# A two-block transformer kernel with a stream of experts: TensorE's pieces of projections and mixers ahead of each step's value products

## The chip, the cores and the metric

The kernel runs on one core of one Trainium2 chip. The metric is the device time of one execution in microseconds; three runs of the kernel before gave 2456.52 to 2461.20 us, with a median of 2458.12.

A core has five engines with instruction queues of their own: TensorE (PE), VectorE (DVE), ScalarE (ACT), GpSimd (POOL) and SyncE (SP). They meet through semaphores. Each executes its own program in order, so an instruction that waits holds up everything behind it on its engine.

## What is computed

Two blocks follow each other on 256 tokens of width 1024. The first mixes a convolution and a recurrent layer, the second has two layers, one with gated linear attention (GLA) and one with stick-breaking attention (SB), both with an attention over a memory of 256 rows. Each of the three layers ends in a PEER layer: 8 heads choose 16 of 16384 experts for each token, and each expert is a pair of rows u and v.

```python
q = (xb @ w_q).reshape(TOK_BLOCK, PEER_HEADS, 2, PEER_DHALF)
s = jnp.einsum('thcd,hcnd->thcn', q, sub_keys).astype(jnp.float32)
top_s, top_i = lax.top_k(s, K)
...
u = expert_u[e]
act = jax.nn.gelu(jnp.einsum('td,ted->te', xb, u), approximate=False)
coef = (gate * act.astype(jnp.float32)).astype(xb.dtype)
return jnp.einsum('te,ted->td', coef, expert_v[e])
```

Everything is float32. The chosen rows of u and v are different for every token, so they are gathered: 128 tokens x 128 experts x 8 KB for each half of the tokens and each layer, 805 MB over the three layers.

## The kernel before

After a first phase (`one_tensor` and its like, up to about 300 us) the kernel runs the *stream*: 768 experts, one after the other, in 384 *steps* of two (`GROUP`). 64 steps make a *window* (`WINDOW`): one layer for one half of the tokens. There are six, counted here from 0: windows 0 and 1 are the first block's layer, 2 and 3 the GLA layer's, 4 and 5 the SB layer's. "Step 23 of window 3" is step 3 x 64 + 23 of the stream.

An expert goes through these stations:

- GpSimd gathers u and v of its 128 tokens (1 MB) into one of eight ring slots (`RING`), once the slot's last user is done: `pool.wait_ge(sem("v_used"), e - RING + 1)`, L2086.
- VectorE multiplies u with the tokens and adds up (the dot product, L2007).
- ScalarE takes GELU (L2053), multiplies with the gate (L2059) and writes the coefficient on the diagonal of a 128x128 matrix (L2065, semaphore `diag`), one of four buffers (`DIAGS`), which it may fill once the products of two steps before are done.
- TensorE multiplies the diagonal with the two halves of v and adds to two accumulators (L1977), then counts up `v_used`, which frees the slot. One step is four instructions, of which the trace shows each as two.

*Beside* the stream runs everything that makes the next layer ready: in window w the mixer of the half whose experts were just added, the projection of the queries, and the scores. `beside_tensor`, `beside_vector` and `beside_scalar` are generators that give a slot number ahead of each piece, and `Beside.run(s)` issues all pieces whose number is at most s. Each engine calls it in its own step s: VectorE behind the dot products of the step, ScalarE behind the diagonals, TensorE behind the products. So the slot numbers set the order, and pieces of one number on two engines can wait for each other. `late` is a second such generator, for the first window alone.

In a mixer's window with first slot `base`, what matters here is:

- SB mixer (windows 3 and 4): `memory_tensor` writes the memory's scores into two banks at slot 20, ScalarE's `memory_exp_scalar` (L2254, four exponentials) reads them at slot 23, and TensorE's `values_part(0)` (L1611, weights `in_sb_v`), also at slot 23, takes the same two banks for its output. `sb_scores_tensor` and `sb_above_tensor` (L2714, L2725, L2728) stand at slot 21 for the third group of heads, and ScalarE copies the scores out at slot 22.
- Queries (`queries_tensor`, all of windows 1 to 4): projection j (L1599) at slot 46 + j, ScalarE's copy of it (L1586) one slot later; the scores of a group of keys (L1743) stand in the slot of the copy of the group's last query.
- Row broadcasts (`row_tensor`, L1472), which the layer norms read: at slot 0 of windows, and at step 380 for the last norm.
- At the start of a window VectorE adds the accumulators to the residual (L1525, `peer_added`), and the first products of the window wait for it.
- Softmax of the best scores (L2023 on ScalarE, behind its pieces in every eighth step), which VectorE needs for the gate (L2214).

TensorE works through six further banks (0 to 5) in turn. `banks.take` waits until the bank's last content has been read. Weights come through three slots that SyncE reloads once TensorE has used them.

Of the kernel before, what the change touches and what calls it, by code (L numbers as in the profile page):

```python
# [203 lines left out]
def build(nc, io):  # L204
    with ExitStack() as ctx:  # L205
# [5 lines left out]
        def sem(name):  # L211
            if name not in sems:
                sems[name] = ctx.enter_context(nc.semaphore(name))
            return sems[name]
# [109 lines left out]
        for n in range(len(plan)):  # L324
            s = n % SLOTS if n < stream_from else (n - stream_from) % STREAM_SLOTS
# [1449 lines left out]
        def late_tensor(pe):  # L1775

            for group in range(EARLY_GROUPS):
                lo, hi = FIRST_GROUPS[group]
                for j in range(lo, hi):
                    for part in range(2):  # L1780
                        yield late_slot(group, 2 * (j - lo) + part)
                        if part == 0:
                            pe.wait_ge(*banks.take(("q", 0, j, 1)))
                        out = banks.bank(("q", 0, j, 1))
                        for kc in range(4 * part, 4 * part + 4):
                            ins = nc.tensor.matmul(out[:, 0:P], early_q[:, j, kc * P:(kc + 1) * P], xT[:, kc, cols_of(1)],
                                                   start=kc == 0, stop=kc == KC - 1)
                    ins.then_inc(banks.full_sem(("q", 0, j, 1)), 1)
                yield late_slot(group, 4)
                for j in range(lo, hi):  # L1790
                    pe.wait_ge(*banks.emptied(("q", 0, j, 1)))
                early_scores(pe, group, 1, late_q)
# [171 lines left out]
        def stream_tensor(pe):  # L1964
            beside = Beside(beside_tensor(pe))
            late = Beside(late_tensor(pe))
            beside.run(-1)
            pe.wait_ge(sem("w_o_last_added"), 2)
            for s in range(UNITS // PH * WINDOW):
                if s and s % WINDOW == 0:  # L1970
                    pe.wait_ge(sem("peer_added"), 2 * (s // WINDOW))
                for e in range(s * GROUP, (s + 1) * GROUP):
                    first, last = e % TILE_EXPERTS == 0, e % TILE_EXPERTS == TILE_EXPERTS - 1
                    pe.wait_ge(sem("diag"), e + 1)
                    for half, acc in enumerate((acc_lo, acc_hi)):
                        at = D + 512 * half
                        ins = nc.tensor.matmul(acc[:, :], diag[:, e % DIAGS, :], ring[:, e % RING, at:at + 512],  # L1977
                                               start=first, stop=last)
                        if e == UNITS * PK - 1 and half == 0:
                            ins.then_inc(sem("last_half"), 1)  # L1980
                    ins.then_inc(sem("v_used"), 1)
                beside.run(s)
                late.run(s)
            beside.run(UNITS * PK)

        def stream_vector(v):
# [104 lines left out]
        def beside_tensor(pe):  # L2091
            yield from first_tensor(pe)
            for w in range(4):
                n, i = w // NT + 1, w % NT
                yield from (gla_tensor, sb_tensor)[n - 1](pe, i, WINDOW * (w + 1))
                yield from queries_tensor(pe, n, i, WINDOW * (w + 1))
            for i in range(NT):
                yield WINDOW * (5 + i) - 4 * i
                for which in range(2):
                    row_tensor(pe, 5, i, which)  # L2100
# [813 lines left out]
        @blk.tensor  # L2914
        def _(pe):
            one_tensor(pe)
            stream_tensor(pe)
# [142 lines left out]
```

## Time and profile before

| | us |
|---|---|
| median of three runs | 2458.12 |
| the profiled execution, its time | 2457.63 |
| its span, first to last instruction | 2455.8 |
| TensorE busy (matmul) | 2215.1 |
| VectorE busy | 1663.9 |
| ScalarE busy | 904.5 |
| GpSimd busy | 879.6 |

Busy times are shares of a span in which the engines work beside each other; they can't be added. The gathers take 78.5% of what sixteen DMA engines could do in the span, the loads of weights 13.4%. "PE" is the matrix product and "PEld" the loading of its stationary operand, which lies beside it. In a timeline each row is a run of equal instructions: start, length, engine, line, operation, and in brackets the idle time of the engine ahead of it with what ended it. A granted clock of 1.00 is TensorE at 2.4 GHz, and 0.5 would be 1.2 GHz throughout.

### The profile page before, as it was taken

The page shows a single profiled execution, that of the slowest core. Times are in us where ns is not written, and L with a number is a line of the kernel's source. Part 1 is how long each engine was busy: PE and PEld are TensorE (multiplying, and loading weights), DVE is VectorE, ACT ScalarE, POOL GpSimd, SP SyncE. Part 2 cuts the span into 40 slices and gives each one's busy share as a digit, 9 for nine tenths or more (in the row PEclk, how much of TensorE's full clock was granted, in tenths as well). Part 3 has the DMA queues.
Part 4 walks back from the last instruction along what each step waited for, and adds up shares of the span by engine and source line. Part 5 has one row for each costly group of instructions (what it writes and reads, how often), then busy time and mean ns, then how long its engine had stood idle before and what let it go on. Part 6 is the DMA issues. An engine that isn't in the chain of part 4 may idle for free. (4 is left out here: it accounts for less than half of the span.)

```text
span 2455.8 us, 29961 instructions
## 1 busy us (share of the span) xinstructions
PE 2215.1 (90%) x9826; PEld 1270.1 (52%) x9826; DVE 1663.9 (68%) x3980; ACT 904.5 (37%) x2654; POOL 879.6 (36%) x796
## 2 busy tenths in 40 slices
PE   9989999989998889998989987899999999977777
PEld 7877755544554435654545644445655445622223
DVE  3864576666675677666777656767678767676765
ACT  2232133332343434343443424424344534433332
POOL 0012044444433334433344432344443344444442
PEclk9999999999999999999999999999999999999999
DMA  5321699999999999999999999999999999999997
GB/s 198 129 70 33 247 379 426 426 426 427 426 424 424 415 418 412 412 425 424 419 402 426 425 425 422 396 423 426 418 425 422 389 422 426 400 420 427 427 427 323
DMA packets 149784, 934.90 MB, mean 381 GB/s; under 512 B 16656, under 2 KB 18800, under 8 KB 51200
## 3 DMA queue, kind: packets, MB, share of 16 engines
q0 software_dynamic: 110592, 805.36, 78.5%
q1 hardware_dynamic: 39040, 127.65, 13.4%
q8 instruction: 79, 1.29, 0.2%
q14 instruction: 73, 0.60, 0.1%
HBM read 931.89 MB, written 1.05 MB: 380 GB/s over the span
## 5 line engine op out<-in xcount | busy, mean ns | idle before, releaser
L1977 PE MATMUL bank<-arena 128*128 128x512 f32 x3072 | 1425.2, 608 | 196.6 <-ACT arena L2065 193.3
L2086 POOL DMA_INDIRECT arena<-in_uv,idx x768 | 851.9, 1109 | 1359.3 <-PE bank L1977 1218.3
L1977 PEld LDWEIGHTS bank<-arena 128*128 128x128 f32 x3072 | 566.5, 193 | 889.2 <-issue 582.3
L2007 DVE CUSTOM_DVE_ANT_0 arena<-arena,h 128x1024 f32<-128x1024 f32 x512 | 627.4, 1226 | 351.0 <-DMA arena<-in_uv,idx 346.9
L2053 ACT ACTIVATE arena<-arena 128x2 f32<-128x2 f32 x383 | 77.8, 203 | 1046.8 <-DVE arena L2007 1046.3
L2007 DVE CUSTOM_DVE_ANT_0 arena<-arena 128x1024 f32<-128x1024 f32 x256 | 313.8, 1226 | 192.5 <-DMA arena<-in_uv,idx 190.9
L2065 ACT ACTIVATE arena<-const,arena 128x128 f32<-128x128 f32 x766 | 260.0, 386 | 2.2 <-PE bank L1977 2.2
L378 PEld LDWEIGHTS bank<-xT,weights 128*128 128x128 f32 x1360 | 196.5, 191 | 40.6 <-issue 23.5
L378 PE MATMUL bank<-xT,weights 128*128 128x128 f32 (+2 forms) x1360 | 214.8, 314 | 0.0
L2059 ACT ACTIVATE arena<-arena 128x1 f32<-128x1 f32 x766 | 184.3, 288 | 12.5
L1586 ACT ACTIVATE arena<-bank 128x128 f32<-128x128 f32 (+4 forms) x158 | 46.9, 306 | 172.6 <-PE bank L1599 115.3
L2053 ACT ACT_TABLE_LOAD x73 | 93.7, 1283 | 1.3
L1388 POOL TENSOR_TENSOR arena<-arena 128x512 f32<-128x512 f32 (+1 forms) x16 | 17.9, 1125 | 190.5 <-DVE arena L1206 162.9
L2007 DVE DVE_READ_ACCUMULATOR2_ANT arena<- 128x1 f32 x768 | 63.2, 82 | 0.0
L2023 ACT ACT_TABLE_LOAD x48 | 61.6, 1283 | 0.8
L1611 PE MATMUL bank<-weights,xT 128*128 128x256 f32 (+1 forms) x128 | 47.8, 503 | 15.2 <-DMA weights<-in_sb_v 9.4
L1611 PE MATMUL bank<-weights,arena 128*128 128x512 f32 x128 | 60.0, 594 | 0.0
L1108 DVE SCALAR_TENSOR_TENSOR arena<-arena,rows 128x256 f32<-128x256 f32 x120 | 47.6, 478 | 0.0
L1611 PEld LDWEIGHTS bank<-weights,xT 128*128 128x128 f32 x128 | 23.6, 192 | 43.4 <-issue 22.5
L2214 DVE RECIPROCAL arena<-arena 128x1 f32<-128x1 f32 x48 | 7.8, 163 | 54.9 <-ACT arena L2023 54.7
L617 PE MATMUL bank<-arena 64*64 64x64 f32 (+1 forms) x1104 | 37.2, 218 | 6.0 <-DVE arena L1234 4.9
L1599 PEld LDWEIGHTS bank<-xT,held 128*128 128x128 f32 x320 | 38.6, 192 | 7.7 <-issue 7.7
(349 smaller groups left out, 1994.5 us busy)
## 6 DMA issues: line engine op xcount, KB each, us to landing
weights<-in_w_in SPq DMA_DIRECT2D x38, 512.0 KB, 3.5
weights<-in_a_fm SPq DMA_DIRECT2D x28, 512.0 KB, 8.8
arena<-in_uv,idx POOLq DMA_INDIRECT x768, 13.1
arena<-in_w_q SPq DMA_DIRECT2D x16, 512.0 KB, 14.7
weights<-in_w_q SPq DMA_DIRECT2D x16, 512.0 KB, 8.7
weights<-in_a_out SPq DMA_DIRECT2D x16, 512.0 KB, 8.6
weights<-in_b_fm SPq DMA_DIRECT2D x16, 512.0 KB, 8.9
weights<-in_b_out SPq DMA_DIRECT2D x16, 512.0 KB, 8.1
```

The costliest lines, as they stand in the source:

```text
L378: ins = nc.tensor.matmul(out[:, 0:n], w[:, kc * P:(kc + 1) * P], x[:, kc, :], start=kc == 0, stop=kc == KC - 1)
L1108: V.scalar_tensor_tensor(ycv[:, c, :], glu[:, c, bass.ds(tap + META, TOK)], cols[:, bass.ds(tap * CT + (w0 + c), 1)], ycv[:, c, :], ALU.mu ...
L1586: nc.scalar.activation(to, out[0:to.shape[0], 0:n], ACT.Copy, scale=scale).then_inc(banks.emptied_sem(job), 1)
L1599: ins = nc.tensor.matmul(out[:, 0:P], w[:, kc * P:(kc + 1) * P], xw[:, kc, :], start=kc == 0, stop=kc == KC - 1)
L1611: ins = nc.tensor.matmul(banks.bank((name, i, half))[:, 0:hw], x, slot((name, i, kc))[:, 512 * half:512 * half + hw], start=first, stop=last)
L1977: ins = nc.tensor.matmul(acc[:, :], diag[:, e % DIAGS, :], ring[:, e % RING, at:at + 512], start=first, stop=last)
L2007: V.tensor_tensor_reduce(out=u, in0=u, in1=x, scale=1.0, scalar=0.0, op0=ALU.mult, op1=ALU.add, accum_out=dots[:, unit % 2, kx:kx + 1]).th ...
L2023: ins = nc.scalar.activation(expo, best, ACT.Exp, bias=tiny[:, 0:1], accum_out=tiny[:, 1:2])
L2053: nc.scalar.activation(actv[:, par, kx:kx + GROUP], dots[:, par, kx:kx + GROUP], ACT.Gelu).then_inc(sem("gelu"), 1)
L2059: nc.scalar.activation(coef[:, par, j:j + 1], actv[:, par, j:j + 1], ACT.Copy, scale=gate[:, par, j:j + 1]).then_inc(sem("coef"), 1)
L2065: nc.scalar.activation(diag[:, (e + j) % DIAGS, :], ident, ACT.Copy, scale=coef[:, par, kx + j:kx + j + 1]).then_inc(sem("diag"), 1)
L2086: nc.gpsimd.indirect_dma_start(out=ring[:, s, :], out_offset=None, in_=io[f"uv{unit // PH // NT}"], in_offset=bass.IndirectOffsetOnAxis(ap ...
```

## The change

In each step of `stream_tensor` the two calls that issue the pieces move from behind the products to the head of the step, ahead of the wait for `peer_added` too. The other engines' programs stay as they are.

```diff
@@ -1967,6 +1967,8 @@
             beside.run(-1)
             pe.wait_ge(sem("w_o_last_added"), 2)
             for s in range(UNITS // PH * WINDOW):
+                beside.run(s)
+                late.run(s)
                 if s and s % WINDOW == 0:
                     pe.wait_ge(sem("peer_added"), 2 * (s // WINDOW))
                 for e in range(s * GROUP, (s + 1) * GROUP):
...
                     ins.then_inc(sem("v_used"), 1)
-                beside.run(s)
-                late.run(s)
             beside.run(UNITS * PK)
```

The products' line is L1977 before and L1979 after. On TensorE around step 23 of window 3, before: the last two instructions of the products of step 22, those of step 23, the first values piece, and the first half of the products of step 24.

```order
L1977 MATMUL bank<-arena 128x512 [waits diag]
L1977 MATMUL bank<-arena 128x512
L1977 MATMUL bank<-arena 128x512 [waits diag]
L1977 MATMUL bank<-arena 128x512
L1977 MATMUL bank<-arena 128x512 [waits diag]
L1977 MATMUL bank<-arena 128x512
L1611 MATMUL bank<-weights,xT 128x512 [waits emptied_4,landed_2]
L1611 MATMUL bank<-weights,xT 128x256 [waits emptied_5]
L1611 MATMUL bank<-weights,xT 128x512 [waits landed_0]
L1611 MATMUL bank<-weights,xT 128x256
L1977 MATMUL bank<-arena 128x512 [waits diag]
L1977 MATMUL bank<-arena 128x512
```

The same place after: the end of the products of step 22, the first values piece, the products of step 23, and the start of the second values piece.

```order
L1979 MATMUL bank<-arena 128x512 [waits diag]
L1979 MATMUL bank<-arena 128x512
L1611 MATMUL bank<-weights,xT 128x512 [waits emptied_4,landed_2]
L1611 MATMUL bank<-weights,xT 128x256 [waits emptied_5]
L1611 MATMUL bank<-weights,xT 128x512 [waits landed_0]
L1611 MATMUL bank<-weights,xT 128x256
L1979 MATMUL bank<-arena 128x512 [waits diag]
L1979 MATMUL bank<-arena 128x512
L1979 MATMUL bank<-arena 128x512 [waits diag]
L1979 MATMUL bank<-arena 128x512
L1611 MATMUL bank<-weights,xT 128x512 [waits landed_1]
```

The piece with its waits for `emptied_4` and `emptied_5`, which ScalarE's exponentials (L2254) count up, has moved ahead of the products of its step.

On TensorE from the end of window 4 into window 5, before: the scores piece behind the last products of window 4, the first products of window 5, and the row broadcasts for the norm.

```order
L1743 MATMUL bank<-weights,arena 128x128 [waits emptied_3,emptied_4,emptied_2,emptied_5,emptied_1,landed_0]
L1743 MATMUL bank<-weights,arena 128x128 x3
L1977 MATMUL bank<-arena 128x512 [waits diag,peer_added]
L1977 MATMUL bank<-arena 128x512
L1977 MATMUL bank<-arena 128x512 [waits diag]
L1977 MATMUL bank<-arena 128x512
L1472 MATMUL bank<-row_parts,const 128x128 [waits emptied_0,rows_in]
L1472 MATMUL bank<-row_parts,const 128x128 x3
L1472 MATMUL bank<-row_parts,const 128x128 [waits emptied_1]
L1472 MATMUL bank<-row_parts,const 128x128 x3
```

The same place after.

```order
L1743 MATMUL bank<-weights,arena 128x128 [waits emptied_3,emptied_4,emptied_2,emptied_5,emptied_1,landed_0]
L1743 MATMUL bank<-weights,arena 128x128 x3
L1979 MATMUL bank<-arena 128x512 [waits diag]
L1979 MATMUL bank<-arena 128x512
L1979 MATMUL bank<-arena 128x512 [waits diag]
L1979 MATMUL bank<-arena 128x512
L1472 MATMUL bank<-row_parts,const 128x128 [waits emptied_0,rows_in]
L1472 MATMUL bank<-row_parts,const 128x128 x3
L1472 MATMUL bank<-row_parts,const 128x128 [waits emptied_1]
L1472 MATMUL bank<-row_parts,const 128x128 x3
```

The scores now stand ahead of the last products of window 4, and the row broadcasts ahead of the first of window 5, which still wait for `peer_added`.

## Rows read from the trace of the kernel before

**Rows 1.** Page, 40 slices: busy tenths of PE and DMA, and GB/s.

```profile
PE   9989999989998889998989987899999999977777
...
DMA  5321699999999999999999999999999999999997
GB/s 198 129 70 33 247 379 426 426 426 427 426 424 424 415 418 412 412 425 424 419 402 426 425 425 422 396 423 426 418 425 422 389 422 426 400 420 427 427 427 323
```

**Rows 2.** Table of waits, whole run: total us, times, longest us.

```profile
POOL arena L2086 <- PE bank L1977: 1218.3, 698, 7.2
...
PE bank L1977 <- ACT arena L2065: 193.3, 163, 4.6
...
ACT arena L1586 <- PE bank L1599: 115.3, 62, 3.8
```

**Rows 3.** Gathers (L2086) of 2160:2400, then 1550:1595, 1925:1965, 2090:2150.

```profile
DMA to landing us min/median/max: 11.4/12.6/14.8
...
DMA to landing us min/median/max: 6.8/10.8/14.2
...
DMA to landing us min/median/max: 6.3/8.1/10.4
...
DMA to landing us min/median/max: 5.9/8.4/11.7
```

**Rows 4.** Windows: length, busy PE PEld DVE ACT POOL, clock, DMA share, GB/s.

```profile
1570.00:1600.00 30.00, 28.48 (x101) 14.36 (x102) 17.55 (x45) 11.33 (x32) 8.87 (x9) 1.00 0.97 368
1900.00:1960.00 60.00, 57.20 (x196) 29.67 (x194) 47.79 (x105) 32.43 (x79) 20.36 (x17) 0.97 0.97 387
2110.00:2160.00 50.00, 46.88 (x191) 27.02 (x190) 39.49 (x97) 20.24 (x64) 20.84 (x20) 1.00 0.99 385
2049.28:2135.23 85.95, 85.47 (x402) 54.67 (x400) 56.46 (x141) 32.43 (x109) 35.65 (x33) 1.00 1.00 412
```

**Rows 5.** Timeline of PE, steps 22 to 26 of window 3.

```profile
1539.82 3.70 PE L1977 MATMUL bank<-arena 128*128 128x512 f32 x8 [0.28 <-ACT arena L2065]
1545.67 5.40 PE L1977 MATMUL bank<-arena 128*128 128x512 f32 x8 [2.16 <-ACT arena L2065]
1550.91 2.74 PE L1611 MATMUL bank<-weights,xT 128*128 128x512 f32 x8
1553.49 3.60 PE L1977 MATMUL bank<-arena 128*128 128x512 f32 x8
...
1559.62 1.56 PE L1611 MATMUL bank<-weights,xT 128*128 128x512 f32 x4 [1.24 <-DMA weights<-in_sb_v]
1561.01 3.60 PE L1977 MATMUL bank<-arena 128*128 128x512 f32 x8
1566.59 1.56 PE L1611 MATMUL bank<-weights,xT 128*128 128x512 f32 x4 [1.99 <-DMA weights<-in_sb_v]
...
1571.38 3.60 PE L1977 MATMUL bank<-arena 128*128 128x512 f32 x8
```

**Rows 6.** Timeline of ACT, window 3: last of four exponentials at step 23.

```profile
1548.59 0.48 ACT L2254 ACTIVATE arena<-bank,small 128x256 f32<-128x256 f32 x1
```

**Rows 7.** Windows, L1977 alone: length, busy PE PEld, clock, DMA share, GB/s.

```profile
1545.60:1551.10 5.50, 5.40 (x8) 2.03 (x8) 0.69 1.01 426
```

**Rows 8.** Timeline of PE, window 2, behind a longer wait.

```profile
1237.53 9.45 PE L1977 MATMUL bank<-arena 128*128 128x512 f32 x16 [4.59 <-ACT arena L2065]
```

**Rows 9.** Timeline of ACT, window 4, step 22: copies of the scores.

```profile
1904.24 1.09 ACT L1586 ACTIVATE arena<-bank 128x512 f32<-128x512 f32 x2 [4.61 <-PE bank L2714]
```

**Rows 10.** Timelines of DVE and PE, end of window 4 and start of 5.

```profile
2105.49 0.16 DVE L2214 RECIPROCAL arena<-arena 128x1 f32<-128x1 f32 x1 [5.44 <-ACT arena L2023]
...
2138.77 3.73 PE L1472 MATMUL bank<-row_parts,const 80*128 80x128 f32 x32
```

**Rows 11.** Timeline of PE, the last three steps.

```profile
2437.41 10.46 PE L1977 MATMUL bank<-arena 128*128 128x512 f32 x24
```

**Rows 12.** Timeline of PE, window 0, piece of step 2.

```profile
340.66 1.10 PE L394 MATMUL bank<-xT,weights 128*128 128x256 f32 x4 [0.72 <-DVE xT L1578]
```

## The prediction

> **What bounds the kernel now.** I read the page first, by its slices. Over almost the whole stream of experts the DMA engines are busy in every slice and move about 426 GB/s; TensorE shows nine tenths or more in most slices beside them [rows 1]. The table of waits says how they hang together: a gather waits for TensorE's product (L1977) 698 times, and the product waits for ScalarE's diagonal (L2065) for 193.3 us in all [rows 2]; between the two lies VectorE's dot product. It is a ring of eight slots, so two things can set the end: the bytes, or the ring, when TensorE releases a slot so late that the DMA queue runs empty.
>
> Which one it is can be read from a gather's time from issue to landing. In the last window, where TensorE has no other work, it is 11.4 to 14.8 us and the slices move 427 GB/s: the queue is full, bytes are the bound. Where the rate falls, the time does too: 6.8 to 14.2 us from 1550 to 1595, 6.3 to 10.4 from 1925 to 1965, and 5.9 to 11.7 from 2090 to 2150 [rows 1, 3]. I take 8 us, near the low ends and the median of 8.1 in the leanest stretch, as the time of a gather that finds no queue ahead of it; what a stretch shows above that is its cover, the time by which a release may come late at no cost. The three stretches in which the rate falls most move 368 GB/s over 30 us, 387 over 60 and 385 over 50 [rows 4]. Against 427 that is 30 x 59/427 = 4.1 us, 60 x 40/427 = 5.6 us and 50 x 42/427 = 4.9 us: some 15 us are lost to the ring, and no more can be won there. A later release costs time only where cover is gone, and there it costs nearly its own length.
>
> **What the change does to TensorE.** Nothing is added or removed, and the other four engines keep their rows. In the program, each step's pieces now stand behind the products of the step before and ahead of its own. Since products and pieces alternate either way, most steps look alike: TensorE did pieces s-1 and then waited for diagonal s; now it does pieces s in the same gap. Two things differ. First, ahead of products s there now lies piece s instead of piece s-1, so where TensorE has no idle time, products s start later by (piece s minus the piece that last fell into idle time), and earlier where the next piece is short. Second, ScalarE does its own part of step s behind diagonal s. A piece that needs that part used to have 3.6 us of products as cover; now TensorE stands still for it with the products queued behind, and the release of two slots behind them. By the semaphores I find such pieces at steps 22 of windows 1 and 2, at 20, 23 and 27 of windows 3 and 4, at the five groups of scores in each of windows 1 to 4, and at five places of window 0. The other way round, ScalarE's copy of step s+1 no longer waits for products s.
>
> **The sum, place by place.** Times are of the profiled execution (span 2455.8, its time 2457.63; the median of the three runs is 2458.12, so I add 0.5).
>
> *Window 3, step 23.* The value projection's first piece takes the two banks that ScalarE's four exponentials of the memory read. These run behind the diagonal of step 23 and end at 1548.59 + 0.48 = 1549.1. The products before end at 1539.82 + 3.70 = 1543.5, and the diagonal is ready when the next start, at 1545.67 [rows 5, 6]. Now TensorE stands until 1549.1, does the piece (2.74 us), and the products start near 1551.8, 6.1 us later, and end at 1555.4 instead of 1551.1. The pieces behind it are long: from the end of one step's products to the start of the next 3.9 us (1557.1 to 1561.0) and 6.8 us (1564.6 to 1571.4), with waits of 1.24 and 1.99 us for weights in them [rows 5]. They now lie ahead of products 24 and 25 instead of 25 and 26. Carrying the times forward so gives releases later by 4.3, 5.7, 8.6, 7.1, 4.5 and 2.7 us for steps 23 to 28. The weights' own chain (use, reload, use) moves with the pieces, which I have counted as half of its waits saved. Cover at these steps, each gather's time to landing less 8 us, is about 5, 5, 6, 3, 1 and 0 us; its two ends are those of the stretch [rows 3]. So the queue runs dry by 0, 1, 3, 4, 3.5 and 3: **3.5 us**, not given back, since from there the bytes bind again.
>
> The clock adds to it. The eight product records took 5.40 us there, behind 2.16 us of idle, and 3.6 a step later; the granted clock of that stretch is 0.69, so a part of it went at 1.2 GHz, for 1.8 us more. Behind 4.59 us of idle in window 2 sixteen records took 9.45 us instead of 7.2, 2.25 more [rows 5, 7, 8]. The new idle time is 5.6 us, and the piece behind it goes at the low clock too, so I take up to 2 us more and half of it as reaching the end: **1 us**. The Trainium skill (TensorE: Matmul & The Clock Gate, "Why this matters for your kernels") wants no long idle gaps of TensorE between bursts, since its clock goes back to half rate behind one. If only the new, longer gap counted as one, the whole 1.8 us would be new and the term 1.8; the row shows the fall at 2.16 us of idle time already, and I go by the row.
>
> *Window 4, the same step.* Here ScalarE itself waited 4.61 us for TensorE's scores of the step before, and its copies came at 1904.24 [rows 9]. That piece now goes ahead of its products, so ScalarE is about 3 us earlier, its exponentials end near 1908.5, and TensorE arrives at that time: no stall. What is left is the order: releases later by 3, 6, 2.4, 4.4, 4, 1.4 and 3.2 us, cover 3, 4, 0.5, 2, 0.5, 0 and 0. Carried through, **1.7 us**.
>
> *End of window 4.* From 2049.28 to 2135.23 TensorE is busy for 85.47 of 85.95 us: in this stretch it sets the pace, in either order [rows 4]. The last idle time before it lies at a step with a short piece, so the 1.6 us piece of each step now comes ahead of its products and releases move back by 1.0 us. Behind the window's end the four broadcasts of the norm's rows (3.4 us) precede the first products instead of following them: that release is 2.4 us later, the next 1.1 us earlier [rows 10]. Cover is nil there: **1 us**. VectorE's 5.44 us wait for the softmax (it came because ScalarE's copy stood behind a piece that stood behind products) goes away, but TensorE is late there by more [rows 10]; nothing is gained.
>
> *The start.* Piece 2 of window 0 waits for VectorE's transposes, in place at 340.66 [rows 12]; its products now start near 341.5 instead of 336.3. The ring has just been filled there, and a release 5 us late uses its cover up to within 1 us; I take **0.3** (0 to 1.5). The five score groups of window 0, and those of windows 1 and 2 with step 22, stall TensorE by 1 to 5 us, over cover of 4 us or more and with idle time behind them: nought, at most 1 us in all.
>
> *The tail.* The norm rows (3.4 us) stood behind the products of step 380 and left the last three steps back to back, 2437.41 to 2447.87 [rows 11]. Now they use 1.2 us of idle time ahead of them; only the last expert's diagonal, ready by 2445.0, binds: **-0.6 us**.
>
> Sum: 3.5 + 1 + 1.7 + 1 + 0.3 - 0.6 = 6.9, so 2457.63 + 6.9 + 0.5 = **2465.0 us**. The uncertain terms reach from nothing to about twice their size (0 to 9 for window 3, 0 to 4 each for window 4 and its end), 0 to 17 in all.
>
> **Rivals.** *A, the cover holds* (2457 to 2462): emptier gather queues let the weights land sooner, and these are what TensorE waits for in windows 3 and 4; the pieces shrink as the releases slip. For it: waits for weights in just these pieces [rows 5]. Against: the diagonal of step 23 and the exponentials don't move. Price: 0 to 4 us. *B, faster* (about 2451): ScalarE's copies wait 115.3 us for TensorE's projections [rows 2], and no longer behind products. If ScalarE and VectorE being early shortens the loop from landing to release, half of the 15 us comes back: 2458.1 - 7.3 = 2450.8. It decides where products start with their diagonal; in the starved stretches they start 3 us and more behind it, which speaks against it. *C, much slower* (2470 to 2476): late products hold up ScalarE's diagonals (four buffers), so its parts, and again TensorE's pieces, and stalls grow round the loop in windows 1 to 4: 3 us in each, +12 to +18.
>
> **How the numbers follow.** The forecast of some 3 to 12 us has 0.52, A 0.30, B 0.12, C 0.06. A measurement of this kernel tells 0.2%, 4.9 us, from no change: below 2453.2 is faster (B), above 2463.0 slower (C and nine tenths of the forecast): faster 0.12, same 0.35, slower 0.53. For 8 in 10 the range goes from 2454, between B and A, to 2474, the upper end of the terms.
>
> **What the profile will show.** Right: in window 3 step 23 TensorE idle for over 5 us ahead of the L1611 piece, waiting for ScalarE (L2254), a longer low clock; GB/s lower around 1570 to 1610; ScalarE's waits for L1599 much smaller; VectorE's 5.4 us wait gone; about 85.5 us of TensorE work from step 48 to the window's end. Wrong if that idle time is there and the landings are not later (A), or if the three lean stretches move more than 400 GB/s (B).

## The result and the profile after

The changed kernel took 2464.77 us (median of 13 runs, 2461.57 to 2471.00), beside 2457.87 for the kernel before (13 runs, same chip). The ratio is 1.0033, with a 95% interval of 1.0025 to 1.0041: slower by 6 to 10 us. The profiled execution took 2465.51 us, its span is 2463.7.

The page after, 40 slices (busy tenths of PE and DMA, and GB/s):

```profile
PE   9989999999998889998989987899999999977777
...
DMA  5320689999999999999999999999999999999997
GB/s 197 128 70 28 246 353 426 426 426 426 426 414 423 421 402 420 407 425 424 419 411 426 426 424 422 392 424 426 416 422 422 377 425 426 398 423 427 426 427 331
```

Hardly anything stands out beside [rows 1]: the slices are tens of microseconds wide, and the loss is 7 us in 2464. The sixth slice, in which the stream starts, moves 353 GB/s instead of 379, in part because the first gather of this execution landed 2.7 us later, and the one in the middle of window 4 (from 1909 us) 377 instead of 389. The table of waits (total us, times, longest us) tells more:

```profile
POOL arena L2086 <- PE bank L1979: 1212.6, 680, 10.4
...
PE bank L1979 <- ACT arena L2065: 159.5, 137, 4.8
...
DVE arena L2214 <- ACT arena L2023: 33.8, 36, 2.2
...
ACT arena L2065 <- PE bank L1979: 17.8, 19, 1.3
...
PE bank L1743 <- ACT rows L1586: 10.3, 5, 2.6
...
PE bank L378 <- ACT arena L2254: 9.7, 2, 6.0
...
ACT arena L1586 <- PE bank L1599: 7.6, 11, 1.3
...
PE bank L2232 <- ACT arena L1586: 7.1, 2, 3.7
...
PE bank L1611 <- ACT arena L2254: 4.9, 1, 4.9
```

The products (now L1979) wait 34 us less for their diagonals than in [rows 2], and ScalarE's copies 7.6 us instead of 115.3 for the projections. The four lines of PE behind L1743 (the score groups of window 0), L378 (step 22 of windows 1 and 2), L2232 and L1611 (steps 20 and 23 of the SB mixer) are new: TensorE stands still for ScalarE work of its own step, with the products queued behind. Such a wait in front of a moved piece is called a stand below. The longest single wait of a gather for its slot rises from 7.2 to 10.4 us. What the pieces saved was idle time that cost nothing; what they now wait for lies on the ring. Which of the stands cost time is a question of cover, and the experiments answer it.

Window 3 after, timeline of PE, steps 22 to 26, the counterpart of [rows 5], and ScalarE's last exponential ([rows 6]):

```profile
1545.65 3.70 PE L1979 MATMUL bank<-arena 128*128 128x512 f32 x8
1554.22 5.41 PE L1611 MATMUL bank<-weights,xT 128*128 128x512 f32 x8 [4.87 <-ACT arena L2254]
1559.47 3.60 PE L1979 MATMUL bank<-arena 128*128 128x512 f32 x8
...
1565.48 3.60 PE L1979 MATMUL bank<-arena 128*128 128x512 f32 x8
...
1572.08 1.56 PE L1611 MATMUL bank<-weights,xT 128*128 128x512 f32 x4 [1.71 <-DMA weights<-in_sb_v]
1573.48 3.60 PE L1979 MATMUL bank<-arena 128*128 128x512 f32 x8
...
1578.89 1.56 PE L1611 MATMUL bank<-weights,xT 128*128 128x512 f32 x4 [0.53 <-DMA weights<-in_sb_v]
```

```profile
1554.42 0.48 ACT L2254 ACTIVATE arena<-bank,small 128x256 f32<-128x256 f32 x1
```

The stand of the forecast is there, with its owner (4.87 us, 5.6 forecast), and the piece behind it takes 5.41 us instead of 2.74. From products 22 to products 23 it is 13.8 us now and 5.85 before.

Windows of after: the three lean stretches of [rows 4] moved by the delay that has built up until there, and TensorE's full stretch from step 48 of window 4 to the first products of window 5 (length, busy PE PEld DVE ACT POOL, clock, DMA share, GB/s):

```profile
1576.00:1606.00 30.00, 29.47 (x104) 14.55 (x103) 18.10 (x47) 11.88 (x31) 12.44 (x11) 1.00 0.99 387
1908.00:1968.00 60.00, 56.50 (x179) 28.39 (x179) 45.03 (x98) 32.59 (x76) 21.87 (x18) 0.97 0.95 373
2118.00:2168.00 50.00, 47.23 (x181) 26.65 (x181) 37.16 (x91) 18.25 (x57) 21.58 (x20) 0.97 0.99 394
2059.17:2146.39 87.22, 87.22 (x419) 56.43 (x417) 58.42 (x145) 31.43 (x108) 36.87 (x33) 1.00 1.00 408
```

The first of them moves more than it did before the change (387, against 368), the second less (373, against 387).

### The profile page after: what moved, and what is told of

Its sections match the earlier page's. It is cut to its first block and busy times, and to the rows that moved or that the text cites. A ratio compares the mean times of both kernels' runs of the same rounds, so it can differ in the third digit from the quotient of the medians.

```text
span 2463.7 us, 29961 instructions
## 1 busy us (share of the span) xinstructions
PE 2222.7 (90%) x9826; PEld 1278.5 (52%) x9826; DVE 1664.1 (68%) x3980; ACT 895.0 (36%) x2654; POOL 888.4 (36%) x796
## 5 line engine op out<-in xcount | busy, mean ns | idle before, releaser
L1979 PE MATMUL bank<-arena 128*128 128x512 f32 x3072 | 1423.6, 608 | 160.5 <-ACT arena L2065 159.5
L2086 POOL DMA_INDIRECT arena<-in_uv,idx x768 | 860.7, 1121 | 1357.9 <-PE bank L1979 1212.6
L1979 PEld LDWEIGHTS bank<-arena 128*128 128x128 f32 x3072 | 569.5, 194 | 847.5 <-issue 580.9
L2065 ACT ACTIVATE arena<-const,arena 128x128 f32<-128x128 f32 x766 | 261.5, 387 | 17.8 <-PE bank L1979 17.8
L378 PE MATMUL bank<-xT,weights 128*128 128x128 f32 (+2 forms) x1360 | 218.4, 318 | 12.3 <-ACT arena L2254 9.7
L378 PEld LDWEIGHTS bank<-xT,weights 128*128 128x128 f32 x1360 | 199.5, 194 | 53.9 <-issue 36.9
L2059 ACT ACTIVATE arena<-arena 128x1 f32<-128x1 f32 x766 | 184.3, 288 | 12.5
L1611 PE MATMUL bank<-weights,xT 128*128 128x256 f32 (+1 forms) x128 | 50.6, 531 | 17.3 <-DMA weights<-in_a_v 6.7
L1611 PE MATMUL bank<-weights,arena 128*128 128x512 f32 x128 | 60.0, 594 | 0.0
L1611 PEld LDWEIGHTS bank<-weights,xT 128*128 128x128 f32 x128 | 25.0, 202 | 46.4 <-issue 28.8
L394 PE MATMUL bank<-xT,weights 128*128 128x256 f32 x160 | 40.5, 380 | 3.3 <-DVE xT L1578 3.3
L1599 PEld LDWEIGHTS bank<-xT,arena 128*128 128x128 f32 x320 | 38.6, 192 | 7.6 <-issue 7.6
## 6 DMA issues: line engine op xcount, KB each, us to landing
arena<-in_uv,idx POOLq DMA_INDIRECT x768, 12.5
```

The costliest lines, as they stand in the source:

```text
L378: ins = nc.tensor.matmul(out[:, 0:n], w[:, kc * P:(kc + 1) * P], x[:, kc, :], start=kc == 0, stop=kc == KC - 1)
L394: ins = nc.tensor.matmul(out[:, 0:n], w[:, kc * P:(kc + 1) * P], x[:, kc, :], start=kc == 0, stop=kc == KC - 1)
L1611: ins = nc.tensor.matmul(banks.bank((name, i, half))[:, 0:hw], x, slot((name, i, kc))[:, 512 * half:512 * half + hw], start=first, stop=last)
L2059: nc.scalar.activation(coef[:, par, j:j + 1], actv[:, par, j:j + 1], ACT.Copy, scale=gate[:, par, j:j + 1]).then_inc(sem("coef"), 1)
L2065: nc.scalar.activation(diag[:, (e + j) % DIAGS, :], ident, ACT.Copy, scale=coef[:, par, kx + j:kx + j + 1]).then_inc(sem("diag"), 1)
L2086: nc.gpsimd.indirect_dma_start(out=ring[:, s, :], out_offset=None, in_=io[f"uv{unit // PH // NT}"], in_offset=bass.IndirectOffsetOnAxis(ap ...
```

## Where the time went, place by place

In most places the bytes hide where a delay starts, so I read every trace at one kind of event: the landing of the second gather of a step. The table gives the time between such landings. The first column ends at step 12, the others at the end of window 0, window 3 step 5, window 3 step 59, window 4 step 45, window 5 step 11, and step 63 of window 5; the sum runs from step 4 of the stream to its last landing. The kernels in the middle are those of the experiments below.

| trace | start | rest of w0 | w1, w2 | w3 | w4 | end of w4 | w5 | sum | median us |
|---|---|---|---|---|---|---|---|---|---|
| before | 41.7 | 271.3 | 765.0 | 322.3 | 287.7 | 155.5 | 256.8 | 2100.3 | 2457.9 |
| before, again | 41.7 | 271.6 | 764.6 | 323.0 | 287.0 | 155.6 | 256.9 | 2100.3 | |
| e1_start | 45.7 | 271.2 | 763.9 | 322.5 | 287.5 | 155.4 | 257.5 | 2103.7 | 2460.3 |
| e2_sb | 41.7 | 271.4 | 764.7 | 324.1 | 288.8 | 155.7 | 256.8 | 2103.2 | 2460.6 |
| e3_rest | 41.7 | 271.3 | 764.8 | 322.7 | 291.4 | 155.3 | 256.8 | 2104.1 | 2459.7 |
| e4_mem_early | 44.0 | 271.1 | 765.4 | 322.3 | 290.9 | 155.3 | 257.1 | 2106.0 | 2461.8 |
| e5_start_fixed | 41.7 | 271.6 | 764.3 | 323.5 | 293.3 | 155.0 | 256.9 | 2106.2 | 2461.7 |
| e6_all_fixed | 41.7 | 271.4 | 765.1 | 322.0 | 286.5 | 155.9 | 256.2 | 2098.7 | 2457.7 |
| e7_hybrid | 41.7 | 272.2 | 765.1 | 321.4 | 291.2 | 154.9 | 256.9 | 2103.5 | 2457.3 |
| after | 44.6 | 271.6 | 766.2 | 322.9 | 290.3 | 155.2 | 256.5 | 2107.4 | 2464.8 |
| after, again | 43.6 | 272.1 | 766.6 | 324.5 | 292.1 | 156.0 | 257.3 | 2112.3 | |

Mean of the two of after less the mean of the two of before: 2.5 + 0.4 + 1.6 + 1.1 + 3.9 + 0.1 + 0 = 9.6 us, and -0.6 for the tail (13.2 to 12.5 us from the last landing to the end); the medians differ by 6.9, so two traces of each overstate the loss by some 2 us. The difference has two main seats, the start and window 4, and window 3 is not one of them. The 1.6 us of windows 1 and 2 are not repeated where the same order stands in them: e3_rest has 764.8 and e5_start_fixed 764.3, with stands of up to 6.3 us at step 22.

## Experiments

**The change cut in three.** One condition decides which steps have their pieces ahead of the products:

```diff
             for s in range(UNITS // PH * WINDOW):
-                beside.run(s)
-                late.run(s)
+                first_here = s < 12
+                if first_here:
+                    beside.run(s)
+                    late.run(s)
...
                     ins.then_inc(sem("v_used"), 1)
+                if not first_here:
+                    beside.run(s)
+                    late.run(s)
```

e1_start has `s < 12`, e2_sb `s // WINDOW in (3, 4) and 16 <= s % WINDOW < 34`, e3_rest the opposite of both.

> Pieces ahead of the products in steps 0 to 11 of the stream alone; everywhere else the order of before. Theory T (a late release costs time only at a few places where the cover is gone): the trace of the changed kernel shows the landings of the gathers 2.0 us later behind step 12 than ahead of step 0, since TensorE's piece of step 2 waits for VectorE's transposes with the products behind it; so 2459.9, +2.0 us against before, and the offset of the landings stays level from step 12 to the end. By the term of the prediction (0.3 us) it would be 2458.2. Rival S (the cost is spread evenly over the 384 steps, some 7 us in all): 12 of 384 steps, +0.2 us.

> Pieces ahead of the products in windows 3 and 4, steps 16 to 33, alone; everywhere else the order of before. Theory T: +3 to +4 us against before (2461 to 2462), +0.9 of it in window 3 and +2 to +3 in window 4, as the landings' offsets in the trace of the changed kernel have it. By the terms of the prediction (3.5 + 1 + 1.7) it would be +6.2 us, 2464.1, most of it in window 3. Rival S (evenly spread): 36 of 384 steps, +0.7 us, 2458.5.

> Pieces ahead of the products in all steps but 0 to 11 and windows 3 and 4, steps 16 to 33: the complement of the two runs before it. Theory T: no place without cover is left but the windows' ends, and the tail gives 0.6 us back, so -0.5 to +1.5 us against before, 2457.4 to 2459.4. By the terms of the prediction (1 for the end of window 4, -0.6 for the tail) +0.4. Rival S (evenly spread): +6 us, 2464.

Beside 35 runs of before with a median of 2457.57: e1_start 2460.30 (ratio 1.0015, 1.0006 to 1.0024), e2_sb 2460.57 (1.0013, 1.0003 to 1.0023), e3_rest 2459.66 (1.0005, 0.9995 to 1.0016). The three shares make 0.33%, the whole again, though each is known to 0.1% only. 12 steps out of 384 carry 0.15 of it, where an even spread gives them 0.01, and e3_rest is 2.1 us above before where it expects 6: the even spread is ruled out. Of theory T's three figures e1_start came out 0.7 us higher than expected in time and 2 us higher in its trace (4.0 at the start), and e3_rest just outside the range of -0.5 to +1.5. Its trace is 3.8 us longer than before's, nearly all of it in window 4 (291.4), though the places where TensorE would stand there have the old order; longer waits for in_sb_v weights (4.3 us from 1880 to 1965, before 2.8) are a part of it. How much window 4 scatters is taken up below. The trace of e1_start shows where, in the timeline of PE at step 2:

```profile
337.64 1.10 PE L394 MATMUL bank<-xT,weights 128*128 128x256 f32 x4 [3.31 <-DVE xT L1578]
338.58 5.29 PE L1981 MATMUL bank<-arena 128*128 128x512 f32 x8
```

The piece waits for VectorE's transposes, which VectorE writes behind its dot products of step 3. The products behind it even go at a lower clock here (5.29 us instead of 3.60). In the trace of after the same wait is 3.33 us and the products take 3.60; e1_start lost 4.0 us up to step 12, after 2.9, for nearly the same idle time. In [rows 12] the piece had products ahead of it and waited 0.72.

e2_sb met the theory's total at its lower end (+3.0 us by the medians), not its split: 1.5 us in window 3 and 1.5 in window 4, where 0.9 and 2 to 3 were expected. The prediction's own 6.2 us lies just above its interval (0.7 to 5.7). Its products of window 3 run late by 6.3, 6.3, 8.7, 5.2, 2.6 and 0.8 us at steps 23 to 28, close to the forecast's own series (4.3, 5.7, 8.6, 7.1, 4.5, 2.7), and the second landings of its steps by at most 4.0; by step 59 1.8 us are left (1.1 against the other trace of before).

**Stands taken away.** e4_mem_early is the changed kernel with the memory's softmax one step earlier in both mixers, which takes the stands at step 22 of windows 1 and 2 and at step 23 of window 3 away together. The SB mixer's edit is shown, the GLA mixer's is alike:

```diff
-            yield o + 24
             memory_exp_scalar(act, 1, i)
...
-            yield o + 23
             memory_max_vector(v, 1, i)
```

> The changed kernel, with ScalarE's exponentials of the memory and VectorE's maximum ahead of them one step earlier in both mixers, so that TensorE's value pieces no longer wait for ScalarE work of their own step. Nothing else moves. If the stand of 5.6 us of TensorE in step 23 of window 3 (and its like at step 22 of windows 1 and 2) is what costs: 1 to 4 us less than the changed kernel, 2461 to 2464. If only the order costs (a long piece ahead of its products rather than behind them), the stand goes from the trace and the time stays at 2464.8 within 1 us.

It took 2461.76 (1.0017, 1.0006 to 1.0028). The stands at steps 22 and 23 are gone from its trace, and window 3 is back at 322.3. e5_start_fixed has `first_here = s >= 3`:

> The changed kernel, with the order of before in steps 0, 1 and 2 of the stream alone, so that TensorE's first piece of the next projection (L394, step 2) again has products ahead of it while VectorE writes its operand. Theory T: the 3.3 us wait in front of that piece is what the start costs, so 2 to 4 us less than the changed kernel: 2461 to 2462.5, landings as early as in the kernel before at step 12. Rival O (the order of steps 3 to 11 costs by itself, since pieces lie ahead of each of their products): at most 1 us less, 2464.

2461.68 (1.0015, 1.0006 to 1.0025), beside 2456.78 for before. The first 12 steps take 41.7 us as before; the order of steps 3 to 11 costs nothing. Both take some 3 us off the median, at the edge of what their intervals tell from the changed kernel.

**The stand at step 20 too.** e4 and e5 kept the cost of window 4, and their traces show a stand there that I had named among the candidates and not costed, TensorE's scores of the memory at step 20 (L2232). Timeline of PE, window 4, steps 20 and 21, before, and then after:

```profile
1890.38 5.40 PE L1977 MATMUL bank<-arena 128*128 128x512 f32 x8 [1.96 <-ACT arena L2065]
1895.71 1.14 PE L2232 MATMUL bank<-arena 64*128 64x256 f32 x8
1896.78 3.70 PE L1977 MATMUL bank<-arena 128*128 128x512 f32 x8
```

```profile
1897.24 2.00 PE L2232 MATMUL bank<-arena 64*128 64x256 f32 x8 [3.40 <-ACT arena L1586]
1899.17 4.49 PE L1979 MATMUL bank<-arena 128*128 128x512 f32 x8
```

The diagonal of this step is late in both orders, since ScalarE is busy with its pieces of the step before (after, two table loads and three activations from 1889.63 to 1895.40). Before, TensorE waited 1.96 us for it, did the products and then the piece. After, the piece waits for ScalarE's copy, which comes behind both diagonals, and so the products start 2.7 us behind the first diagonal (ready near 1896.4 by ScalarE's timeline), which is itself the late event. e6_all_fixed combines both earlier edits with this one:

```diff
-            yield o + 21
+            yield o + 22
             memory_tensor(pe, 1, i)
-            yield o + 22
             sb_above_tensor(pe, 1, i)
```

> The changed kernel with the edits of the two runs before it that took single stands away (order of before in steps 0 to 2; ScalarE's exponentials of the memory and VectorE's maximum one step earlier), and TensorE's scores of the memory in the SB mixer (L2232) one step later, so that they no longer wait 3.4 us for ScalarE's copy of their own step. Theory W (what costs is TensorE standing for ScalarE or VectorE work of the same step, with the products queued behind): the cost of window 4 goes with the stand at step 20, 2457.5 to 2460. Rival O (what costs is the order itself, a long piece ahead of its products where the queue is lean): the cost in windows 3 and 4 stays at 3 to 6 us as in the two earlier kernels without a stand at step 23, 2461 to 2463.

2457.72 (1.0006, 0.9995 to 1.0017), beside 2456.42 of before: the interval lies clear of the changed kernel's 1.0025 to 1.0041. Its PE timeline of the same place:

```profile
1887.67 3.70 PE L1980 MATMUL bank<-arena 128*128 128x512 f32 x8 [2.65 <-ACT arena L2069]
1891.30 1.14 PE L2236 MATMUL bank<-arena 64*128 64x256 f32 x8
```

The pieces that had moved in front of their operands (step 2 of the stream, step 22 of windows 1 and 2, 20 and 23 of windows 3 and 4) together account for most of the cost at least. With eight slots the order in itself, in the other steps, costs nothing that these runs can tell. Nor does a stand as such: e6_all_fixed keeps those of the score groups of window 0, 10.8 us in five waits, and loses nothing there (271.4 for the rest of window 0, before 271.3 and 271.6).

How the cost divides among these pieces is known less well. By the medians the edits of e4 and e5, 3 us each, already make 6 of the 6.9, which leaves next to nothing for step 20; by the traces window 4 has the largest share. And none of these edits was tried on the kernel before, so it isn't shown that they give nothing of their own there; against a large gain speaks e7_hybrid below.

**Less cover.** If a delay costs only where the queue of gathers has run down, a shorter queue must make every delay dearer. In r7_before and r7_after each gather waits for one more release, as if the ring had seven slots; r7_fixed is e6_all_fixed with the same line:

```diff
-                        pool.wait_ge(sem("v_used"), e - RING + 1)
+                        pool.wait_ge(sem("v_used"), e - RING + 2)
```

> The kernel before with a gather waiting for the release of one expert later (L2085), as if the ring had seven slots: each gather is issued about 2.4 us later, so the cover is 2.4 us smaller everywhere. Cover theory: the stretches in which the queue runs dry grow; +10 to +35 us, 2468 to 2493. If bytes alone set the time outside the three lean stretches and these are TensorE's, it stays within 3 us of the kernel before.

> The changed kernel with the same edit. Cover theory: what the changed order delays finds less cover, so the distance from this kernel to its partner (before with the same edit) is larger than the 7 us between the two kernels with eight slots: 12 to 30 us. If the cost of the change isn't a matter of cover, the distance stays at 5 to 9 us.

> The kernel ahead of this one with a gather waiting for one more release, which shrinks the cover by one expert and, in the pair measured before, made 7 us of difference into 18.5. Theory W: with the stands gone the distance to the kernel before with the same edit (2469.8) is 0 to 5 us, so 2470 to 2475. Rival O: most of the distance stays, 2480 to 2486.

| | us | ratio to before | w0, start | w0, rest | w1, w2 | w3 | w4 | end of w4 |
|---|---|---|---|---|---|---|---|---|
| r7_before | 2469.82 | 1.0045 (1.0029 to 1.0061) | 42.5 | 272.3 | 766.2 | 324.5 | 291.9 | 160.9 |
| r7_fixed | 2477.51 | 1.0083 (1.0064 to 1.0103) | 41.9 | 273.8 | 774.3 | 325.7 | 289.7 | 159.2 |
| r7_after | 2488.36 | 1.0122 (1.0108 to 1.0137) | 47.5 | 271.7 | 776.8 | 324.0 | 297.5 | 158.6 |

In the last window the gathers of r7_before land after 10.4 us in the median, where [rows 3] has 12.6:

```profile
DMA to landing us min/median/max: 8.7/10.4/12.8
```

So the cover is 2.2 us smaller. Before loses 13 us by it, and the distance between the two orders grows from 6.9 to 18.5 us, inside what the cover theory expected and far beyond its rival's 5 to 9. The start and window 4 stand out again, 5.0 and 5.6 us, and the edits take both away entirely. But the largest share now lies in windows 1 and 2, 10.6 us, and of it the edits take only 2.5: r7_fixed came out between the two expectations, 7.7 us above r7_before, and its windows 1 and 2 alone are 8.1 us longer. There, with seven slots, the order costs without the stands that were taken away. With eight slots the same windows differ by 0.1 (e6_all_fixed 765.1, before 765.0). One thing the traces show: from 640 to 1420 us a gather's longest wait for its slot is 9.1 us in e6_all_fixed and 9.5 in r7_fixed, but 6.6 before and 6.7 in r7_before. The changed order releases slots less evenly, and eight slots hide what seven don't. What makes it uneven I didn't take apart.

**The noise of one trace.** Both kernels once more:

> The kernel before once more, for its trace: how far one profiled execution differs from the next where nothing is changed. From the first runs: the landing of the first gather scatters by some 3 us either way (first phase, the same program in all kernels), and the time from the first landing to the last, 2124.9 us in the trace of before, comes again within 1.5 us. If it differs by 3 us or more, the terms of 1 to 3 us that I read from single traces are worth nothing.

> The changed kernel once more, for its trace: how far two profiled executions of it differ, place by place. From the pair of before: the time between first and last landing comes again within 1.5 us (2130.6 in the first), the stands of TensorE within 0.5 us, the share of windows 3 and 4 singly within 2 us, since the two traces of before differ by 1.8 us in each of them with opposite sign.

The second trace of before gave 2123.8 us from the first landing to the last instead of 2124.9, and 2100.3 again for the sum above. The second of after gave 2135.3 instead of 2130.6, beyond the 1.5 expected: windows 3 and 4 took 1.6 and 1.8 us more. Its stands in windows 3 and 4 are the same (3.73, 4.87 and 3.40 us). What differs in window 4 is the clock and the wait for weights: behind the same stand of 3.40 us the products of step 20 take 5.57 us instead of 4.49, and the waits for in_sb_v at steps 24 and 26 are 2.88 and 2.11 us instead of 2.22 and 1.28.

**A version better than both?** The trace of e6_all_fixed was 1.6 us shorter than before's, mostly in windows 3 and 4. e7_hybrid keeps the old order up to window 2 and takes e6's from window 3 on.

> The order of before in windows 0 to 2 and the changed order from window 3 on, with the two edits of the SB mixer that take its stands at steps 20 and 23 away; the GLA mixer as before. By the traces so far: windows 0 to 2 as before, windows 3 and 4 as in the kernel with all stands gone, where the transferred bytes run 2.4 us ahead of before, and the tail 0.6 us shorter: 3 us less than before, 2453.5 to 2456. Rival: that gain in windows 3 and 4 is chance between traces (the two traces of before differ by 1.8 us in window 3 and back in window 4): within 1 us of before.

2457.30, beside 2456.81 of before (1.0001, 0.9990 to 1.0011). The rival was right: that gain does not come again. The traces of e6 and e7 show what chance it is. Up to step 23 of window 4 each event of e7 follows the one of e6 at a fixed distance, to 0.1 us. Then, PE ahead of products 24 to 26 in e6_all_fixed, and ahead of products 24 and 26 in e7_hybrid:

```profile
1913.41 1.56 PE L1611 MATMUL bank<-weights,xT 128*128 128x512 f32 x4 [2.19 <-DMA weights<-in_sb_v]
...
1920.49 1.56 PE L1611 MATMUL bank<-weights,xT 128*128 128x512 f32 x4 [0.80 <-DMA weights<-in_sb_v]
...
1927.18 1.56 PE L1611 MATMUL bank<-weights,xT 128*128 128x512 f32 x4 [0.41 <-DMA weights<-in_sb_v]
```

```profile
1917.62 2.93 PE L1611 MATMUL bank<-weights,xT 128*128 128x512 f32 x4 [2.56 <-DMA weights<-in_sb_v]
...
1933.36 1.83 PE L1611 MATMUL bank<-weights,xT 128*128 128x512 f32 x4 [1.86 <-DMA weights<-in_sb_v]
```

The first wait is 0.37 us longer, and the piece behind it goes at a granted clock of 0.50 instead of 1.00, 1.37 us longer. Products 24 are 1.7 us late by that. Ahead of products 26 weights and clock add more, and products 27 of e7 are 4.0 us behind those of e6. So a single trace says little about window 4: the six traces without the stand at step 20 there have 286.5 to 291.4 us, the five with it 288.8 to 293.3. The means, 288.6 and 291.1, differ by 2.5 us, about half of what either group scatters, so the size of this share isn't well known. The medians don't settle it: e6_all_fixed lies 4 us below e4 and e5, but it differs from each of them by two edits.

## Why the prediction was right, and where it wasn't

The total was right: 2465.0 forecast, 2464.8 measured. So was the mechanism: pieces that need work of their own step stand, the releases behind them come late, and that costs where cover is gone. The terms that made up the sum were not all right: window 3 was put too high by about 3 us, the start and, by the traces, window 4 too low by about 2 each, and these cancel. The agreement of the total to 0.2 us is luck.

**Window 3, step 23 (forecast 3.5 for the queue and 1 for the clock, measured 1 to 2).** Stand, clock, series of late releases and the depth of the queue's hole came as worked out; the second landings of the steps were late by up to 4.0 us in e2_sb. The step that failed is "not given back, since from there the bytes bind again". They don't. Before, and then after, windows from products 22 to products 26 and from there to products 31:

```profile
1539.82:1571.38 31.56, 24.34 (x57) 11.01 (x58) 25.91 (x62) 19.02 (x47) 10.30 (x8) 0.95 1.01 421
1571.38:1601.37 29.99, 28.47 (x101) 14.08 (x100) 17.86 (x46) 12.31 (x35) 9.81 (x10) 1.00 0.97 367
```

```profile
1545.65:1581.16 35.51, 28.40 (x73) 14.08 (x73) 27.56 (x66) 20.67 (x50) 9.73 (x10) 0.90 0.99 397
1581.16:1605.91 24.75, 24.75 (x86) 11.83 (x85) 14.51 (x37) 10.37 (x28) 10.94 (x9) 1.00 0.98 379
```

The first part is 4 us longer after, the second 5.2 us shorter. Over both TensorE needs 61.55 us before and 60.26 after, with 8.7 and 7.1 us of idle in them. The new stand of 4.87 us took the place of idle time that stood there anyway: 2.16 us for the diagonal, and waits for weights, which fell from 6.6 to 2.2 us in all, as the loads went on during the stand. The new hole in the queue took the place of the hole that before has a little later, the 4.1 us of [rows 4]: against 427 GB/s the two parts lack 0.4 and 4.2 us of transfer before, and 2.5 and 2.8 after. I had added the one to the other. Rival A had named half of it, the pieces that shrink because the weights are there, and at this place it was largely right. From products 22 to products 39 the four traces with the stand need 104.2 to 104.9 us, the seven without it 101.4 to 104.8, 102.4 in the mean: 2 us. That the rate would fall at 1570 to 1610 was wrong too, for the same reason (387 GB/s, above 368).

**Window 4 (forecast 1.7, "no stall", measured 3.9, some 2.5 of it by the means with and without the stand).** At step 23 there is no stand, as forecast, and ScalarE's copy waits 1.10 us instead of the 4.61 of [rows 9]. Wrong was to cost only step 23 of the three candidates on the list. Step 20 makes TensorE stand 3.40 us, and e6_all_fixed, without that stand, is no slower than before by its interval; its own share stays uncertain, as said above. [Rows 4] could have told: the stretch 1900 to 1960, the longest of the lean ones, begins 10 us behind it, so cover was nearly nil.

**The start (forecast 0.3, measured 2.5).** The time of the late products was right (343.57, 341.5 forecast plus the 2.7 us by which this execution's first landing came later). Mis-sized was the cover. I took the ring as just filled; between products 3 and products 4 the DMA moves 309 GB/s (427 there before), and only from products 6 on 426 again. TensorE needs 4.3 us for a step there and the bytes 4.9, so it makes up 0.6 us in each step, and the products start behind their diagonals until step 7; before, TensorE waits for a diagonal again at step 7 already.

**End of window 4 (forecast 1, measured 0.1).** TensorE is busy for 87.22 of 87.22 us, 1.3 us longer than in [rows 4], since the row broadcasts now precede the first products of window 5, in place of a piece of 1.8 us. (They take 3.7 us by [rows 10], not the 3.4 of the sum.) That part came as forecast; the landings had it back by step 11 of window 5, where before loses as much itself. VectorE's 5.4 us wait is gone, its longest now is 2.2, and it gained nothing, as forecast.

**Windows 1 and 2 (at most 1, measured 1.6)** with stands of 5.98 and 3.75 us at step 22, which e3_rest and e5_start_fixed don't confirm as a cost (764.8 and 764.3 us, before 765.0 and 764.6); **the tail (-0.6, measured -0.6)**: only 0.56 us of idle time ahead of the last two steps' products.

```profile
2448.61 7.13 PE L1979 MATMUL bank<-arena 128*128 128x512 f32 x16 [0.56 <-ACT arena L2065]
```

**The rivals.** B found nothing: the waits of ScalarE's copies for the projections all but vanished and, counted from step 4, no landing of a step came sooner. C (diagonals held up by late products, delays that grow round the loop in each window) occurred in its first step only: ScalarE's diagonals wait for products 17.8 us in all, before 2.2, but never more than 1.3 us at a time, and nothing grows from it; in e2_sb the products of window 3 are 6.3 us late at step 23 and on time at step 31.

The Trainium skill (TensorE: Matmul & The Clock Gate, "Why this matters for your kernels") names long idle gaps as what sends the clock back. Here 1.96 us of idle time were enough at step 20 of window 4 before (5.40 us for the products) and 2.56 us in e7_hybrid, 2.19 us in e6_all_fixed were not, and at the start the products behind 3.31 us (e1_start) went slower and those behind 3.33 us (after) did not. As in the forecast, the rows decide, and by them the length of the gap alone doesn't tell.

## What to carry to other kernels

When work is moved ahead of an instruction that others wait for, look at what each moved piece waits for in the same step: the saved idle time is worth nothing off the critical path, and a few pieces that stand for their own step's work can cost more than all the rest gains. Whether one does depends on the cover where it stands: 3.3 us at the start cost 2 to 4, 6.3 us in window 1 nothing that shows. Cost a delay at its place, and ask whether the kernel loses time there or just behind anyway: a new hole in a queue may take the place of an old one. Moving the few pieces that stand by one step, on either engine, took nearly all of the loss away with eight slots, and about 11 of 18.5 us with seven.

## What the runs showed of the hardware

- Before the stream all kernels run the same program, yet the second landing of its first step came between 318.4 and 325.3 us in the traces. Single runs of one kernel scatter by about 6 us either way, and part of it arises there: the profiled runs with early landings lie below their kernel's median (e4_mem_early 318.4 and -3.3 us, e6_all_fixed 319.6 and -4.5), those with late ones above (e2_sb 325.3 and +2.8, e7_hybrid 323.8 and +4.4). From step 4 on, the two traces of before agree to 0.1 us over 2100, the two of after only to 4.9.
- A stretch in which TensorE waits for weights has more than one outcome with the same instructions. 0.37 us more of such a wait, the fall of the clock behind it and the waits that follow made 4.0 us within three steps.
- One slot of eight is worth 13 us to the kernel before and 24 to the changed one, though the median time from issue to landing falls by only 2.2 us.
